# A layer with PEER experts on one Trainium2 core: three tiles instead of two by indirect DMA, two raw buffers of U in retrieval, and U loaded from GpSimd's queue in the gates

## The reference, cut to what matters

```python
q = (xb @ wq).reshape(T, PEER_HEADS, 2, PEER_DKEY // 2)
s = jnp.einsum('thpk,hpnk->thpn', q, keys)
sv, si = lax.top_k(s, PEER_TOPK)
cand = (sv[:, :, 0, :, None] + sv[:, :, 1, None, :]).reshape(T, PEER_HEADS, PEER_TOPK * PEER_TOPK)
cv, ci = lax.top_k(cand, PEER_TOPK)
...
e = (i1 * PEER_NKEYS + i2).reshape(T, PEER_HEADS * PEER_TOPK)
gate = jax.nn.softmax(cv, axis=-1).reshape(T, PEER_HEADS * PEER_TOPK)
act = jax.nn.gelu(jnp.einsum('ted,td->te', u_tab[e], xb))
coef = (gate * act)
return jnp.einsum('te,ted->td', coef, v_tab[e])
```

## Time and profile before

| | |
|---|---|
| median of three runs | 4409.38 us |
| the profiled execution's own time | 4415.49 us |
| its span, first to last instruction | 4413.8 us |
| TensorE's mean granted clock | 0.964 of full speed |
| PE busy | 4038.8 us (92%) |
| DVE busy | 2919.4 us (66%) |
| ACT busy | 1103.6 us (25%) |
| GpSimd busy | 1063.8 us (24%) |
| moved by DMA | 715.21 MB, mean 162 GB/s |

### The profile page before, as it was taken

One profiled execution on the slowest core, in us unless ns is written; L12 is line 12 of the kernel. 1 busy time (PEld: TensorE's weight loads), 2 busy tenths in 40 slices (PEclk: granted clock), 3 DMA queues, 4 the chain that ended last, 5 costly groups with the idle time before them and its releaser, 6 DMA issues. The chain is left out here.

```text
span 4413.8 us, 63969 instructions
## 1 busy us (share of the span) xinstructions
PE 4038.8 (92%) x22459; PEld 3473.7 (79%) x22459; DVE 2919.4 (66%) x7057; ACT 1103.6 (25%) x1947; POOL 1063.8 (24%) x867
## 2 busy tenths in 40 slices
PE   4999799878897999988999899999999899999996
PEld 3899798866896888878888788888888566666675
DVE  3642344446114989989999288888885566666676
ACT  4543232224111222223333212122221111111112
POOL 0210344422000000000000033333330555555521
PEclk7999899989998999999999999999999999999998
DMA  4111112123312323325767577777772788888844
GB/s 155 34 50 52 66 49 73 39 96 108 105 56 83 111 94 109 111 85 138 189 175 184 181 234 240 243 248 244 244 244 89 287 300 286 303 302 284 299 150 142
DMA packets 461203, 715.21 MB, mean 162 GB/s; under 512 B 253233, under 2 KB 305713, under 8 KB 459185
## 3 DMA queue, kind: packets, MB, share of 16 engines
q1 hardware_dynamic: 380624, 415.60, 29.0%
q0 software_dynamic: 80352, 296.78, 20.0%
HBM read 587.25 MB, written 125.04 MB: 161 GB/s over the span
## 5 line engine op out<-in xcount | busy, mean ns | idle before, releaser
L2311 DVE TENSOR_TENSOR peer_y<-peer_y,stored_pv 128x512 f32<-128x512 f32 x560 | 369.8, 683 | 264.7 <-PE stored_pv L2359 263.7
L2357 PE MATMUL stored_pv<-peer_xh 128*128 128x512 f32 x1120 | 447.4, 400 | 33.2 <-DVE peer_y L2311 18.9
L2358 PE MATMUL stored_pv<-peer_xl,peer_xh 128*128 128x512 f32 x1120 | 438.9, 392 | 0.0
L2359 PE MATMUL stored_pv<-peer_xh,peer_xl 128*128 128x512 f32 x1120 | 437.0, 390 | 0.0
L1776 PE MATMUL topk_pu<-peer_xh,topk_Uh 128*128 128x384 f32 (+1 forms) x864 | 327.8, 379 | 62.8 <-ACT topk_act L1760 36.5
L2478 POOL DMA_INDIRECT peer_y<-in_peer_u_rows,experts_idxU x128 | 162.2, 1267 | 683.7 <-DVE peer_idx L2556 519.8
L1777 PE MATMUL topk_pu<-peer_xl,topk_Uh 128*128 128x384 f32 (+1 forms) x864 | 324.9, 376 | 0.0
L1778 PE MATMUL topk_pu<-peer_xh,topk_Ul 128*128 128x384 f32 (+1 forms) x864 | 324.4, 375 | 0.0
L2357 PEld LDWEIGHTS stored_pv<-peer_xh 128*128 128x128 f32 x1120 | 210.8, 188 | 139.5 <-issue 72.1
L2078 DVE TENSOR_SCALAR gates_scaled<-gates_iota,retrieve_slotT 128x128 f32<-128x128 f32 x896 | 302.6, 338 | 5.9 <-issue 5.9
L2245 POOL DMA_INDIRECT stored_rows<-in_peer_v,peer_idx x256 | 271.4, 1060 | 75.0 <-issue 66.9
(11 more groups left out here) (373 smaller groups left out, 9615.1 us busy)
## 6 DMA issues: line engine op xcount, KB each, us to landing
gates<-gates_G SPq DMA_DIRECT2D x56, 1024.0 KB, 11.1
stored_Vr<-in_peer_v SPq DMA_DIRECT2D x80, 512.0 KB, 6.4
stored_C<-acts SPq DMA_DIRECT2D x80, 448.0 KB, 3.9
stored_G<-gates SPq DMA_DIRECT2D x80, 448.0 KB, 5.1
topk_Ur<-in_peer_u SPq DMA_DIRECT2D x55, 512.0 KB, 3.7
experts_Ur<-in_peer_u SPq DMA_DIRECT2D x48, 512.0 KB, 6.3
experts_Vr<-in_peer_v SPq DMA_DIRECT2D x48, 512.0 KB, 6.0
experts_G<-gates SPq DMA_DIRECT2D x48, 448.0 KB, 5.2
```

Of the source, the lines that this page charges most:

```text
L2311: nc.vector.tensor_tensor(dst, dst, pv[r % RING][:], ALU.add).then_inc(y_added, 1)
L2357: mm(pv[r % RING][:], Ch[p][j][:, t], Vh[p][j][:, cols], start=(j == 0), stop=False)
L2358: mm(pv[r % RING][:], Ch[p][j][:, t], Vl[p][j][:, cols], start=False, stop=False)
L2359: last = mm(pv[r % RING][:], Cl[p][j][:, t], Vh[p][j][:, cols], start=False, stop=(j == 1))
```

## The change

`PICKED` goes from 2 to 3, so six tiles (768 columns, two chunks of 384) are dense. `EXTRA` goes from 5 to 4, so `MADE` = 54 + 18 + 4 = 76: experts has 52 blocks (26 pairs), stored 76 (38 pairs). Indirect DMAs become 384 in each of the two stages; in experts `PER` is 16 and the `ug` ring has 5 buffers, in stored a pair of the first 32 has three groups, after results 3, 6 and 9 of 12, with `VRING` still 3.

In back, ACT no longer copies `h` to `h0`; GpSimd's queue writes the tile to DRAM (`first`) instead, and the next tile's evacuation waits for that DMA. In queries SP loads `first` back, and the turning into rows moves from the start of the stage to behind the first quarter of the query matmuls. In retrieval `Ahead` gets two raw buffers, and ACT's Exp moves behind the GELU of block 4. In the gates U stays with one raw buffer, but its loads leave SP's queue for GpSimd's.

```diff
-PICKED = 2
+PICKED = 3
...
+                if 0 <= t - 2 < PICKED:
+                    pool.wait_ge(h_act, 4 * (t - 1))
+                    pool.wait_ge(h_dve, 4 * (t - 1))
+                    pool.dma_start(dram["first"][t - 2], h[:].rearrange("p k c -> p (k c)")).then_inc(first_out, 16)
...
-                    if t - 2 < PICKED:
-                        nc.scalar.activation(h0[:, t - 2], h[:], ACT.Copy).then_inc(first_kept, 1)
...
-                    sp.wait_ge(rows_made, 2 * PICKED)
-                    sp.dma_start(dram["rows"], rows[:].rearrange("p g a b -> p (g a b)")).then_inc(rows_out, 16)
+                    for g in range(PICKED):
+                        sp.dma_start(h0[:, g, :], dram["first"][g]).then_inc(first_in, 16)
+            sp.wait_ge(rows_made, 2 * PICKED)
+            sp.dma_start(dram["rows"], rows[:].rearrange("p g a b -> p (g a b)")).then_inc(rows_out, 16)
...
+                if g == 0:
+                    pe.wait_ge(first_in, 16 * PICKED)
+                    for n in range(PICKED * KB):
+                        if n % GH == 0 and n // GH >= 4:
+                            pe.wait_ge(rows_made, n // GH - 3)
+                        last = nc.tensor.transpose(ps[n // GH % 4][:, n % GH * P:(n % GH + 1) * P], h0[:, n // KB, n % KB * P:(n % KB + 1) * P], core.ident[:])
...
-    def load(self, sp, n):
-        sp.wait_ge(self.u_split, n + 1)
-        sp.dma_start(self.Ur[:], self.dram["peer_u"][n + self.first]).then_inc(self.u_in, 16)
+    def load(self, queue, n, at):
+        if not (isinstance(n, int) and n + 2 - self.raws <= 0):
+            queue.wait_ge(self.u_split, n + (2 - self.raws))
+        i = at % self.raws
+        queue.dma_start(self.Ur[i][:], self.dram["peer_u"][n + self.first]).then_inc(self.u_in[i], 16)
...
-EXTRA = 5
+EXTRA = 4
...
-            ahead.load(sp, 0)
+            ahead.load(sp, 0, 0)
+            ahead.load(sp, 1, 1)
             with sp.Fori(0, TILES) as t:
                 for b in range(A):
-                    ahead.load(sp, t * A + (b + 1))
+                    ahead.load(sp, t * A + (b + 2), b)
                     ahead.store(sp, t * A + b)
...
-                    if b == 2:
+                    if b == A - 2:
                         act.wait_ge(exp_in, t + 1)
...
+            for n in range(RAWS):
+                ahead.load(pool, n, n)
+            with pool.Fori(0, DENSE) as t:
+                for n in range(A):
+                    ahead.load(pool, t * A + (n + RAWS), n)
+            for n in range(RAWS, max(EXTRA, RAWS)):
+                ahead.load(pool, DENSE * A + n, n)
...
                 for n in range(A):
-                    ahead.load(sp, t * A + n + 2)
                     ahead.store(sp, t * A + n)
...
             for j in range(EXTRA):
-                if j + 2 < EXTRA:
-                    ahead.load(sp, DENSE * A + j + 2)
                 ahead.store(sp, DENSE * A + j)
```

More of the change, by code:

```diff
@@ L1272, in _, with stage_back @@
                     last.then_inc(pe_s[s], 1)
-def stage_back(core, xh, xl, h0):
+def stage_back(core, xh, xl):
     nc, dram = core.nc, core.dram
@@ L1580, in _, with stage_queries @@
                     turn_x(t - 1)
-def stage_queries(core, xh, xl, h0):
+def stage_queries(core, xh, xl):
     nc, dram = core.nc, core.dram
@@ L1663, in _ @@
                             high(i // PERW + 1)
+                if g == 0:
+                    for n in range(2 * PICKED):
+                        act.wait_ge(rows_turned, n + 1)
+                        nc.scalar.activation(rows[:, n // 2, n % 2, :], ps[n % 4][:], ACT.Copy).then_inc(rows_made, 1)
         @block.vector
@@ L1687, in _ @@
             mm = nc.tensor.matmul
[L1688 to L1693, removed]
             i = 0
@@ L1726, with __init__ @@
 class Ahead:
-    def __init__(self, core, st, ring, first, xh, xl):
+    def __init__(self, core, st, ring, raws, first, xh, xl):
         self.nc, self.dram, self.ring, self.first, self.xh, self.xl = core.nc, core.dram, ring, first, xh, xl
-        self.Ur = st.sb("Ur", [P, KB, P])
+        self.raws = raws
+        self.Ur = [st.sb(f"Ur{i}", [P, KB, P]) for i in range(raws)]
         self.Uh = [st.sb(f"Uh{i}", [P, KB, P], F32R) for i in range(ring)]
@@ L1749, in store, with high @@
             sp.dma_start(self.dram["acts"][n + self.first][:, chunk(c)], self.act[c][:, 0:width(c)]).then_inc(self.act_out[c], 16)
-    def high(self, act, n, slot):
-        act.wait_ge(self.u_in, 16 * (n + 1))
+    def high(self, act, n, at):
+        i, slot = at % self.raws, at % self.ring
+        act.wait_ge(self.u_in[i], 16 // self.raws * (n - i) + 16)
         act.wait_ge(self.u_made, NTU * (n + 1))
-        self.nc.scalar.activation(self.Uh[slot][:], self.Ur[:], ACT.Copy).then_inc(self.u_high, 1)
+        self.nc.scalar.activation(self.Uh[slot][:], self.Ur[i][:], ACT.Copy).then_inc(self.u_high, 1)
     def gelu(self, act, n, chunks=range(NTU)):
@@ L1760, in gelu, with low, products @@
             self.nc.scalar.activation(self.act[c][:, 0:width(c)], self.pu[c][:, 0:width(c)], ACT.Gelu_apprx_tanh).then_inc(self.gelu_done, 1)
-    def low(self, dve, n, slot):
+    def low(self, dve, n, at):
+        i, slot = at % self.raws, at % self.ring
         dve.wait_ge(self.u_high, n + 1)
-        self.nc.vector.tensor_tensor(self.Ul[slot][:], self.Ur[:], self.Uh[slot][:].bitcast(F32), ALU.subtract)\
+        self.nc.vector.tensor_tensor(self.Ul[slot][:], self.Ur[i][:], self.Uh[slot][:].bitcast(F32), ALU.subtract)\
             .then_inc(self.u_split, 1)
-    def products(self, pe, n, slot, c, half=None):
+    def products(self, pe, n, at, c, half=None):
+        slot = at % self.ring
         mm = self.nc.tensor.matmul
@@ L1831, in stage_topk @@
         R = TOPK_RING
-        ahead = Ahead(core, st, R, 0, xh, xl)
+        assert A % 2 == 0 and A % R == 0
+        ahead = Ahead(core, st, R, 2, 0, xh, xl)
         LOW_AT = [i * 7 // A for i in range(A)]
@@ L1987, in _ @@
                 ahead.gelu(act, t * A + (A - 1))
-                ahead.high(act, t * A + (A + 1), 1 % R)
+                ahead.high(act, t * A + (A + 1), 1)
                 ahead.gelu(act, t * A + A)
@@ L2003, in others @@
                     for c in range(NTU):
-                        ahead.products(pe, t * A + b, b % R, c)
+                        ahead.products(pe, t * A + b, b, c)
             def turn(t):
@@ L2060, in _ @@
                 .then_inc(iota_done, 1)
+            for n in range(RAWS):
[5 more added lines that the diff above has]
+                ahead.load(pool, DENSE * A + n, n)
+            for i in range(RAWS):
+                pool.wait_ge(ahead.u_in[i], 16 * ((DENSE * A + max(EXTRA, RAWS) - i + RAWS - 1) // RAWS))
         @block.vector
@@ L2771, in build @@
             picked = pr.sb("picked", [P, 2, FIRST])
-            with Stage(core, "first") as fs:
-                h0 = fs.sb("h0", [P, PICKED, KB, P])
-                stage_back(core, xh, xl, h0)
-                stage_queries(core, xh, xl, h0)
+            stage_back(core, xh, xl)
+            stage_queries(core, xh, xl)
             with Stage(core, "retrieve") as rt:
```

46 lines of the change are left out of this document (27 added, 19 removed).

## The result

The changed kernel takes 4339.4 us (median of 4 runs, 4335.7 to 4348.7) against 4410.5 for the kernel before on the same chip: a ratio of 0.984 with a 95% interval of 0.9821 to 0.986. The sign of the forecast is right and its size is not: 71 us of the 211 came, and 4339 lies outside 4140 to 4275.

A forecast was written before the change was run, and what follows sets the result against it. Retrieval bound by DVE and PE waiting on each other, gates by DVE, experts and stored by PE. Back and queries +6, retrieval -46, gates -85, experts -1, stored -85 make -211 us: 4198 us, range 4140 to 4275.

The forecast's parts named there:

- the sum for experts: Experts: DVE's 32.4 us a pair becomes 35.4 with added dots, bounding the stage over PE's 33.0; -1 us for the stage.
- the five fetch buffers give each fetch 7 us or more against a landing of 5.0 us: Experts: fetched rows land within the time that five buffers allow, so fetches do not hold up the 35.4 us pair.
- the forecast's own bound of +30: Experts: upper bound of the stage's -1 us, if a fetch's landing costs DVE 1.2 us a pair.
- Slower than before: the fetches' landing: Rival for experts: fetches landing in 12 us or more make the kernel slower, about 4460 us at 12.5; chance 0.04.
- the stall at a pair's head: Stored: PE's wait of about 1 us a pair for an addition goes, since 12 results divide by a ring of 6.
- The choice of 23.3: Stored: us a pair, taken between PE's 22.5 and the earlier 24.2; it gave -85 us for the stage.
- the DMA-bound rival: Rival for stored: at 350 GB/s DMAs make a pair 25.5 us, +70 us, 4268 us in all; chance 0.15.
- GpSimd's queue starves: Rival for the gates: U lands only once DVE runs dry, 6 us per loop block, +107 us, 4305 us; chance 0.06.
- The tail: Gates, behind the loop: fewer, shorter U blocks, not queued behind SP's stores, take +44 us instead of +66.6; gain 22 us.
- retrieval, by its mechanism too: Retrieval: earlier loads of U end DVE's 45.6 us of waits for ACT's high half, -46 us; DVE is then the bound.
- PE's pace by columns: A matmul's time goes by columns: 0.173 us for 384, 0.227 for 512; a 768-column U block takes 8.3 us.
- the forecast's own lower bound: Queries: +3 us of a forecast +6, if copies and turning overlap from the first group on.

The follow-up runs named there:

- e1: The changed kernel with experts' loads put into SP's queue in the order in which their waits are met, same bytes: 4250.0 us, ratio 0.9646.
- e9: e1 with eight fetch buffers in experts in place of five: 4230.7 us, ratio 0.9605.
- e6: The kernel before the change, with e1's new order of experts' loads: 4405.0 us, ratio 1.0001.
- e12: The changed kernel with e7's load orders in experts and stored, e9's eight fetch buffers and e4's loads of U from SP's queue: 4186.1 us, ratio 0.9494.
- e7: e1 with stored's loads in SP's queue also in the order of their waits, V ahead of C: 4218.0 us, ratio 0.9574.
- e11: The changed kernel with SP's loads put in the order of their waits in stored alone: 4306.9 us, ratio 0.9783.
- e4: The changed kernel with U in the gates loaded from SP's queue again, as in the kernel before: 4333.5 us, ratio 0.9825.
- e5: The changed kernel with one raw buffer of U in retrieval and ACT's Exp back behind block 2: 4377.0 us, ratio 0.9913.
- e8: e1 with every fourth dot in experts replaced by a copy of one element, all rows still fetched: 4195.2 us, ratio 0.9525.
- e2: The changed kernel, queue order kept, with experts' fetches after the first five bringing 512 of 1024 elements: 4246.1 us, ratio 0.964.
- e3: The changed kernel with stored's fetches after the first three groups bringing 512 of 1024 elements: 4289.9 us, ratio 0.9745.

## Why the prediction was wrong

**The step that failed** is the sum for experts, 32.4 us of DVE a pair, in which the only wait is that DVE "waits 7.8 us for ACT's high half of U, which stays". That wait did stay, at 0.4 us apiece, in e1 and e9 as in the kernel before, and e6, which issues U earlier, has the same 7.8 us: it tells nothing of U's load. What the sum put at nothing is the landing of U itself. I added four fetches a pair and priced their landing, not what they do to the landing of U beside them, which had 0.7 us to spare. I never read SP's queue in experts; the second G block ahead of U stands plainly in it. In its place the runs show a late U in every pair: experts +93 us where -1 was forecast, 75 of it gone with the order of the loads alone (e1).

**A second step of the same sum** failed by less: "the five fetch buffers give each fetch 7 us or more against a landing of 5.0 us". In e1 the fetches land in 5.6 to 5.8 us in the median, and DVE waits 1.2 us a pair for them, the price of the forecast's own bound of +30; experts is then 18 us longer than before. Only with eight buffers is it shorter, by 16 us (e9) and 14 (e12).

**Where a rival touched it.** "Slower than before: the fetches' landing" named a late landing, but on the wrong transfer. In the changed kernel the fetches landed in 5.6 us and cost 0.3 us a pair; U landed late. Experts and stored both missed the forecast by one mechanism, a load issued behind another's later wait, and none of my rivals had it.

**Stored.** PE's 22.5 us a pair and the end of the stall at a pair's head were right (22.7 in e7). The choice of 23.3 rested on "nothing but the DMAs stands against it"; the order of V's loads stood against it, as e7 and e11 show. In the changed kernel the first 32 pairs run from 3425.0 to 4197.1, 772 us where 746 was forecast, and the six pairs without groups take 17.1 us each where 16.4 was forecast (16.3 in e7): 26 and 4 of the 30 us missing. Entry and end took the 15.2 us of the forecast. The 25.5 us of the DMA-bound rival did not come.

**Gates.** A tile less was worth 56.0 us, not 62.8: six tiles take 383.6 us, from 1948.42 to the split at 2332.05, where seven took 439.6. The rival "GpSimd's queue starves" came true for two issues of 18, with waits of 5.9 and 4.8 us, and that is the difference: without them six tiles take 375.7 us, 62.6 each (e4, and e1 with the loads on GpSimd's queue). The earlier trace rows did not carry over from 128x32 operands to 128x128 ones, as the forecast noted that it might not. The tail fell by 16 us, not 22 (66.6 to 50.6); the queue's part of that was 1 to 2 us by e4, where I had counted 7.

**Right:** retrieval, by its mechanism too (e5); DVE as the bound of experts once U and the fetched rows come in time, 34.8 us a pair against 35.4; PE's pace by columns.

**Right by luck:** queries and back, +6.7 where +6 was forecast. From PE's first query product to its first product of retrieval it is 263.2 us before and 266.5 after, so 3.3 of the 6.7 lie in queries, the forecast's own lower bound. The rest lies ahead, where profiles of one and the same code differ by more: that first product comes at 1116.2 in the kernel before and at 1120.8 in e6, whose code is the same up to there.

The errors, in us: experts 94, stored 30, gates 13, queries 1, and 3 the other way in retrieval, 135 in all, the difference between the 211 forecast and 76 in the spans. Two slips in the forecast's arithmetic are too small to matter: 12 x 1.36 is 16.3 and not 16.4 us, and PE's pace throughout experts, 24 x 2.4 us less, would have been -59 and not -56 us.

## What to carry to other kernels

For each DMA queue, write the loads of one turn of the loop in a row with the time at which each one's wait is met; a load that stands behind a later wait is issued late, and putting the row in the order of those times, at equal bytes, took 75 us off one stage and some 40 off another. Where a change adds traffic, price the landing of every load beside it against the slack that each has now, from its issue to its use. That no engine waits for a load today does not show that slack: here it was 0.7 us. A cut in bytes can't tell a full DMA from a late issue, since it helps both; a change of order at equal bytes can.

## What the runs showed of the hardware

- GpSimd's DMA issue beside DVE's unbroken 128x128 TENSOR_SCALARs mostly takes 0.54 to 0.69 us, and sometimes up to 19.39. In ten profiles of kernels with the loads there, 21 of 180 issues in the loop took 2.4 us or more; all 21 were a tile's third load. Ten took 19.39 and ended 0.12 to 0.13 us after DVE's row had run out. The other eleven, of 2.40 to 16.43 us, ended while the row went on, each 0.12 to 0.20 us after the end of one of its operations, as this one in e8:

```profile
1987.79 13.70 POOL L1762 DMA_DIRECT2D gates_Ur<-in_peer_u  x1 [20.37 <-DVE gates_Ul L1784]
...
2001.07 0.29 DVE L2111 TENSOR_SCALAR gates_one<-gates_iota,retrieve_slotT 128x128 f32<-128x128 f32 x1
2001.26 0.35 DVE L2112 TENSOR_SCALAR gates_scaled<-gates_iota,retrieve_slotT 128x128 f32<-128x128 f32 x1
```

So DVE need not run dry for GpSimd to get through. Three of the profiles (e1, e2, e3) had no long issue; they come from one chip (13 in the runs' records), from which no other profile with these loads is recorded, so whether the chip matters is not shown. Why that place and why only sometimes stays open.

- One core's DMAs carried 393 GB/s over 650 us, fetches of 4 KB rows among them.
- The landing of 512 KB grew with what was issued just ahead of it: U's median is 6.4 us before, 9.2 in the changed kernel (11.3 behind a G block and two V blocks) and, in e1 with nothing issued together with it, 5.5 us, though e1 moved more in the same time.
- PE, which stood for 4.5 us behind DVE in each pair of experts (89.0 us in 20 pieces), came back at a granted clock of 0.50 (1.2 GHz) for the window from 2858 to 2863 and had 1.00 (2.4 GHz) again from 2864, in the windows above. Over the stage the mean is 0.93, against 0.99 before and 1.00 in the window of e9, where the wait is gone.
